# Prologue of a two-block transformer kernel: the first conditioning tiles in buffers of their own, their sums shared between TensorE and VectorE

## The reference, cut to what matters

```
c_act = jax.nn.silu(c)                          # (1, 1024)
mod = c_act @ w_ada[l] + b_ada[l]               # 6 x 1024 columns
sh1, sc1, gt1, sh2, sc2, gt2 = split(mod, 6)
h = rms_norm(x, norm1[l]) * (1.0 + sc1) + sh1
proj = h @ w_in[l]                              # the first large matmul
```

## Time and profile before

| | |
|---|---|
| median of 3 runs | 3449.75 us (3446.74 to 3453.58) |
| the profiled execution | 3449.55 us, of which the span in the trace is 3448.0 us |
| PE busy | 3332.4 us (97%), PEld 2752.0 us (80%) |
| DVE, ACT, POOL busy | 1887.3, 1107.1, 109.6 us |
| first dense matmul (L455) starts | 48.12 us into the span |
| mean granted clock of PE | 0.981 of full |

### The profile page before, as it was taken

How to read it: one execution, slowest core, us unless ns; L and a number is a source line. 1 busy time by engine, 2 the same in 40 slices (tenths; PEclk the granted TensorE clock), 3 DMA queues, 4 the chain that set the end, 5 groups by cost and what they waited for, 6 DMA issues and landing times.

```text
span 3448.0 us, 45974 instructions
## 1 busy us (share of the span) xinstructions
PE 3332.4 (97%) x15492; PEld 2752.0 (80%) x15492; DVE 1887.3 (55%) x2746; ACT 1107.1 (32%) x1465; POOL 109.6 (3%) x151
## 2 busy tenths in 40 slices
PE   5999999999999999999999999989999999999998
PEld 4788887888887788887888888668788878877887
DVE  7354557554446355577544443556575633566655
ACT  3233333322222333343322233253232323432322
POOL 1000000000000000000000000020000001000000
PEclk7999999999999999999999999999999999999999
DMA  6236424422222155325232222102222222012222
GB/s 224 68 122 207 140 91 148 145 92 97 97 97 87 48 172 183 123 92 195 92 103 94 96 77 84 63 25 75 97 91 98 92 94 89 32 62 97 92 92 79
DMA packets 98237, 357.84 MB, mean 104 GB/s; under 512 B 11104, under 2 KB 11120, under 8 KB 97856
## 3 DMA queue, kind: packets, MB, share of 16 engines
q1 hardware_dynamic: 97344, 353.73, 30.7%
q0 software_dynamic: 768, 2.47, 0.2%
HBM read 354.06 MB, written 2.10 MB: 103 GB/s over the span
## 4 chain that ended last, share of the span: by engine, by line
PE 84%; DVE 8%; DVEq 3%; issue 2%; ACT 2%; DMA 1%; ACTq 0%; SPq 0%; POOLq 0%
PE pb L428 22%; PE pb L429 21%; PE pb L430 21%; PE pb L491 2%; PE pb L492 2%; PE pb L493 2%; PE pb L455 2%; PE pb L456 1%; PE pb L459 1%; DVEq L1730 1%; PE pb L573 1%; DMA raw<-stream 1%; PE pb L506 1%; PE pb L873 1%; DVE act L1731 1%
## 5 line engine op out<-in xcount | busy, mean ns | idle before, releaser
L1331 DVE TENSOR_TENSOR lo<-raw,hi 128x1024 fp32r<-128x1024 f32 x549 | 681.6, 1246 | 449.9 <-ACT hi L938 386.6
L428 PE MATMUL pb<-hH,hi 128*128 128x512 f32 x2208 | 865.7, 392 | 13.9 <-DVE lo L1331 10.7
L429 PE MATMUL pb<-hL,hi 128*128 128x512 f32 x2208 | 862.7, 391 | 0.0
L430 PE MATMUL pb<-hH,lo 128*128 128x512 f32 x2208 | 862.1, 390 | 0.0
L938 ACT ACTIVATE hi<-raw 128x1024 fp32r<-128x1024 f32 x549 | 577.6, 1055 | 698.9 <-PE pb L430 417.3
L428 PE MATMUL pb<-yH,hi 128*128 128x512 f32 x1344 | 526.7, 392 | 23.8 <-DVEq L1385 21.1
L429 PE MATMUL pb<-yL,hi 128*128 128x512 f32 x1344 | 525.4, 391 | 0.0
L430 PE MATMUL pb<-yH,lo 128*128 128x512 f32 x1344 | 525.2, 391 | 0.0
L428 PEld LDWEIGHTS pb<-hH,hi 128*128 128x128 f32 x2208 | 416.3, 189 | 102.1 <-issue 6.8
L430 PEld LDWEIGHTS pb<-hH,lo 128*128 128x128 f32 x2208 | 416.3, 189 | 86.5
L429 PEld LDWEIGHTS pb<-hL,hi 128*128 128x128 f32 x2208 | 416.4, 189 | 85.1
(11 more groups left out here) (284 smaller groups left out, 3415.2 us busy)
## 6 DMA issues: line engine op xcount, KB each, us to landing
raw<-stream SPq DMA_DIRECT2D x664, 512.0 KB, 3.3
x<-xT SPq DMA_DIRECT2D x1, 2048.0 KB, 9.3
outT<-act SPq DMA_DIRECT2D x8, 256.0 KB, 2.2
tab<-decay SPq DMA_DIRECT2D x1, 1024.0 KB, 5.5
scr<-ws POOLq DMA_DIRECT2D x2, 256.0 KB, 4.3
scr<-bs POOLq DMA_DIRECT2D x2, 256.0 KB, 4.8
tab<-tables POOLq DMA_DIRECT2D x1, 512.0 KB, 4.0
cst<-consts SPq DMA_DIRECT2D x1, 302.0 KB, 3.3
```

Of the source, the lines that this page charges most:

```text
L428: pe.matmul(out, whi, ahi, start=first, stop=False)
L429: pe.matmul(out, whi, alo, start=False, stop=False)
L430: return pe.matmul(out, wlo, ahi, start=False, stop=last)
L1331: dve.tensor_tensor(lo[:, s], raw[:, s], hi[:, s].bitcast(F32), ALU.subtract).then_inc(lo_ready, 1)
```

## The change

- The 16 first tiles leave the stream and become an array `first` of their own. Each lands in memory that is unused so early: tiles 0 to 7 in `yF`, 8 to 15 in `act3` behind the squares. None waits for a slot. Each has its own semaphore. SP issues tiles 0 to 7, then 3 dense tiles, then tiles 8 to 15, then the rest of the stream.
- Even tiles of `first` are the transposed scale tiles, summed by DVE as before. Odd tiles are the shift weights in their plain layout, and PE makes a shift column from 8 matmuls, with 128 x 128 of the tile as weights and one column of c_act as moving operand, into PSUM bank 3; DVE copies the 8 columns to `mod`.
- The first norm is summed by PE alone (32 matmuls in place of 12); POOL's part is left out at this place.
- ACT makes the root and the sines before the three `hi`; `round_h` at the head of a layer (both layers) makes hH 0 and 1 before `tick(0)`.

```diff
-TILES = N_FIRST + LAYERS * LAYER_TILES + ...
+TILES = LAYERS * LAYER_TILES + ...
+        def first_at(n):
+            if n < 8:
+                return yF[:, n * TILE:(n + 1) * TILE]
+            return act3[:, KT + 2 * (n - 8):KT + 2 * (n - 8) + 2].rearrange("p a s -> p (a s)")
 ...
             sp.dma_start(x[:], xT).then_inc(x_in, 16)
             freed = Count()
-            early = N_FIRST + 3 * RING
+            for n in range(DENSE_AT):
+                sp.dma_start(first_at(n), first[n]).then_inc(first_in[n], 16)
+            early = 3 * RING
             for n in range(early):
+                if n == AHEAD:
+                    for m in range(DENSE_AT, N_FIRST):
+                        sp.dma_start(first_at(m), first[m]).then_inc(first_in[m], 16)
                 sp.wait_ge(lo_ready, freed.next())
                 sp.dma_start(raw[:, n % RING], stream[n]).then_inc(landed[n % RING], 16)
 ...
-            sum_squares()
+            sq.next(KT)
 ...
             spread_c()
-            norm_sum(start=True)
+            def shift_column(k):
+                pe.wait_ge(first_in[2 * k + 1], 16)
+                for j in range(KT):
+                    ins = pe.matmul(pb[:, 3, k:k + 1], first_at(2 * k + 1)[:, j * P:(j + 1) * P], cs[:, 1, j:j + 1],
+                                    start=j == 0, stop=j == KT - 1)
+                return ins
+            norm_sum(start=True, pooled=False)
+            for k in range(KT):
+                ins = shift_column(k)
+            ins.then_inc(shift_full, 1)
 ...
-            def round_h(shift=None):
+            def round_h(shift=None, tick_at=None):
                 for k in range(KT):
+                    if k == tick_at:
+                        tick(0)
                     act.wait_ge(h_scaled, hs.next())
 ...
-            for s in range(AHEAD):
-                split.next()
-                act.wait_ge(landed[(DENSE_AT + s) % RING], 16 * ((DENSE_AT + s) // RING + 1))
-                act.activation(hi[:, s], raw[:, (DENSE_AT + s) % RING], ACT.Copy).then_inc(hi_ready, 1)
             act.wait_ge(setup_in, 16)
             root(then_tick=False)
 ...
+            for s in range(AHEAD):
+                split.next()
+                act.wait_ge(landed[s], 16)
+                act.activation(hi[:, s], raw[:, s], ACT.Copy).then_inc(hi_ready, 1)
 ...
-                tick(0)
-                round_h(mod[:, 0:8])
+                round_h(mod[:, 0:8], tick_at=2)
 ...
-            for n in range(N_FIRST + AHEAD):
-                d = n - DENSE_AT
-                if 0 <= d < AHEAD:
-                    dve.wait_ge(hi_ready, split.next())
-                    dve.tensor_tensor(lo[:, d], raw[:, n % RING], hi[:, d].bitcast(F32), ALU.subtract).then_inc(lo_ready, 1)
-                else:
-                    m = n if d < 0 else n - AHEAD
-                    dve.wait_ge(landed[n % RING], 16 * (n // RING + 1))
-                    ada_sum(n % RING, mod[:, m:m + 1])
-                if n == 14:
-                    rstd()
+            def scale_column(k):
+                w = first_at(2 * k).rearrange("p (a e) -> p a e", a=2)
+                dve.wait_ge(first_in[2 * k], 16)
+                dve.tensor_tensor_reduce(w, w, c_all, 1.0, 0.0, ALU.mult, ALU.add, mod[:, 8 + k:9 + k])
+            for k in range(4):
+                scale_column(k)
+            rstd()
             for s in range(AHEAD):
+                dve.wait_ge(hi_ready, split.next())
+                dve.tensor_tensor(lo[:, s], raw[:, s], hi[:, s].bitcast(F32), ALU.subtract).then_inc(lo_ready, 1)
                 land[s].next(16)
+            for k in range(4, KT):
+                scale_column(k)
+            dve.wait_ge(shift_full, 1)
+            dve.tensor_copy(mod[:, 0:8], pb[:, 3, 0:8])
+            dve.drain()
             dve.wait_ge(trig, 2)
```

More of the change, by code:

```diff
@@ L33 @@
 N_FIRST = 16
-DENSE_AT = 9
+DENSE_AT = 8
 LAYER_TILES = N_ADA + 8 * 8 + 3 * 16 + 4 + 8 * 7
@@ L37 @@
 FFN2_TILES = 2 * sum(SLABS) + 8 * len(SLABS)
-TILES = N_FIRST + LAYERS * LAYER_TILES + (16 + 8 + 8 + FFN2_TILES) + (12 + 12 + 12 + 4 + FFN2_TILES)
+TILES = LAYERS * LAYER_TILES + (16 + 8 + 8 + FFN2_TILES) + (12 + 12 + 12 + 4 + FFN2_TILES)
 C_ID, C_PERM, C_ONES, C_CAUSAL, C_EDGE = 0, P, 2 * P, 3 * P, 4 * P
@@ L83, in repeat, with build @@
         c.n, c.off = n + k * trips, off
-def build(nc, stream, xT, cvec, pos, consts, decay, tables, vec1, ws, bs, vec2, wf, outT):
+def build(nc, stream, first, xT, cvec, pos, consts, decay, tables, vec1, ws, bs, vec2, wf, outT):
     with ExitStack() as ctx:
@@ L230, in build @@
         landed = [sem(f"landed{s}") for s in range(RING)]
+        first_in = [sem(f"first_in{n}") for n in range(N_FIRST)]
+        shift_full = sem("shift_full")
         hi_ready = sem("hi_ready")
@@ L418, in _ @@
         def _(pe):
-            tiles, banks = Count(4 + N_FIRST), Count()
+            tiles, banks = Count(4), Count()
             h_k, y_k, half_k = Count(), Count(), Count()
@@ L922, in _ @@
             split, done, stf = Count(), Count(4), Count()
-            land = [Count(N_FIRST // RING * 16) for _ in range(RING)]
+            land = [Count() for _ in range(RING)]
             ring = {split: RING, done: RING, **{c: 16 for c in land}}
@@ L2027 @@
     stream = np.concatenate(parts)
-    stream = np.concatenate([ada[0][0:DENSE_AT], stream[0:AHEAD], ada[0][DENSE_AT:N_FIRST], stream[AHEAD:]])
+    first = pairs_of(ada[0][8:16], tiles_t(a["w_ada"][0][:, 0:D]))
     assert stream.shape == (TILES, P, TILE), stream.shape
@@ L2038 @@
     data = {
-        "stream": stream,
+        "stream": stream, "first": first,
         "xT": np.ascontiguousarray(a["x"][0].T.reshape(KT, P, S).transpose(1, 0, 2)),
```

## The result

The changed kernel takes 3465.95 us in the median of six runs (3461.90 to 3467.99), the kernel before 3448.22 in six of the same series; the ratio is 1.0047, 95% interval 1.0036 to 1.0058. It is slower, by 12 to 20 us.

A forecast was written before the change was run, and what follows sets the result against it. PE's dense work was taken to bound the kernel, so the first dense matmul's shift from 48.12 to 61.2 us, mainly PE's 192 half-clock passes, gave +13.1 us: about 3463, range 3457 to 3468.

The forecast's parts named there:

- First tiles without slots: Start: first tiles come at the DMA rate, last landing at 38.1 or 44.0; old bound 44.16 falls by up to 6 us.
- The norm: First norm on PE alone: 64 passes at 0.214 us, done at 25.65, root 27.25, refined 28.3, spread done 30.0.
- Shift columns: PE behind the spread: 128 passes at 0.214 us, 27.4 us, from 30.0 to 57.6, hiding the stream's gain.
- The two readings that decided for 0.214 us a pass: One-column passes: clock stays 0.50 through 5.28 us at 19.73, and falls to 0.50 inside 64 passes from 2050.90.
- Copy and DVE's list: After the columns: copy to 57.85, 1.82 us to first scaled x, 1.56 to the first dense matmul at 61.2.
- Edits at nothing: DVE's other scale columns and lo, the tick behind hH 1, and early ws and bs loads: all costed at 0.
- The rival that the clock comes up: PE's one-column sums reach full clock after 3.6 us: first dense matmul 43.5, time 3443 to 3445; chance 0.09.
- the same dense tiles run in the same order, so I take a shift of that moment as the shift of the end: Whole kernel behind the start: the first dense matmul's shift, +13.1 us, was taken as the end's shift.
- in layer 1 hH already waits for DVE, not for the tick, so nothing changes there: Head of layer 1: moving the tick behind hH 1 was claimed to change nothing.

The follow-up runs named there:

- the run with landing alone: The change with all 16 sums on DVE, ACT's three hi and DVE's three lo ahead of the root: 3445.64 us against 3449.22 before, ratio 0.9991.
- the four traces with wide passes: Shift columns moving 128 copies (3454.78 us), these plus 16 matmuls (3453.01), and all sums on DVE, lists reordered, plus 24 (3442.87) or 34 (3442.55) unused 128-column matmuls.
- its second run: The changed kernel itself, unaltered, run once more: 3465.11 us against 3447.25 for the kernel before, ratio 1.0048.
- the one with POOL's norm: The change with POOL again adding squares 0 to 5 and PE making 12 norm matmuls, not 32: 3464.03 us against 3448.16 before, ratio 1.0042.
- the two with wide columns: The change with each shift-column pass moving 128 copies: 3454.78 us, ratio 1.0015 to before; the same plus 16 matmuls of 128 columns: 3453.01, ratio 1.0008.
- the run with four columns on PE: The change with shift columns 4 to 7 on DVE and 0 to 3 on PE: 3447.95 us against 3448.16 before, ratio 1.0000.
- with PE kept busy: The change with 128-copy shift columns and 16 more 128-column matmuls behind them: 3453.01 us against 3449.22 before, ratio 1.0008.
- the runs with 24 and 34 extra matmuls: All sums on DVE, lists reordered, plus unused 128-column PE matmuls from first tile 12's landing: 24, 3442.87 us, ratio 0.9980; 34, 3442.55, 0.9983 (to before).

## Why the prediction was right

The forecast was slower, 3463 us, with 3457 to 3468; it came out at 3465.95. The mechanism is the one forecast. The loss is 17.7 us where the sum had 13.1: the start came out to 0.3 us, and what is missing lies behind it. Step by step:

- **First tiles without slots.** The last first tile was to land at 38.1, at the latest 44.0. The DMA engines ran at 408 GB/s from 30 to 40 us and had nothing left by 42; in the run with landing alone DVE began the last sum at 39.06 without waiting. Hidden behind PE, as said; and worth 4.5 us, with the two lists put in order, where PE is not in the way.
- **The norm.** Sums from 11.73 to 25.54 (forecast 11.8 to 25.65), spread at 28.26 (28.3).
- **Shift columns.** The term on which all hung: 27.3 us from 30.13 to 57.43, forecast 27.4 from 30.0 to 57.6. The two readings that decided for 0.214 us a pass were right. By the Trainium skill's rule that activity releases the throttle (TensorE: Matmul & The Clock Gate, Part 1) the clock should have come up: PE was busy without a break for 13.8 and for 29.2 us and stayed at 0.50. In the four traces with wide passes the clock did come up, 2.8 to 5.9 us after their start.
- **Copy and DVE's list.** The copy took 0.17 and L1528 began 0.25 behind it, as forecast. From L1528 to the first scaled x it took 2.26 us, not 1.82: 0.66 us idle in front of L1567 where the trace of before had 0.22 at that step. (The same step comes back, larger, below.) DVE was done by 39.5, not 42, which changes nothing. From there to the matmul 1.55 (1.56). First dense matmul 61.53, forecast 61.2.
- **Edits at nothing.** The tick behind hH 1 cost nothing to be seen, ws and bs at 3.2 us did not delay x (it had landed at 11.0, before at 11.1). So the interleaving of loads that the Trainium skill describes (DMA: Bandwidth & Descriptors, Issuing engines are not separate DMA queues) cost x nothing here.
- **The rival that the clock comes up.** It did not, and no run brings it up in one-column passes. Its prices were near what the wide passes took: 0.112 us a pass for its 0.11, and 2.8 to 3.3 us of half speed first (5.9 in one trace) for its 3.6. With the shift columns alone wide the first dense matmul came to 50.21; the rival's 43.5 took both groups of sums at the full clock. One of its sums is off: at 0.14 us a pass the gain is not nil. By its own sum PE makes 200 passes up to the dense work (64, 8 and 128) and the rest of the path is 18.35 us, so the first dense matmul would be at 46.4, and the gain is nil at 0.149.

**What was mis-sized.** The medians differ by 17.7 and 17.9 us, the first dense matmuls by 13.4. So some 3 to 4 us of the loss are not in the chain that was summed: the step "the same dense tiles run in the same order, so I take a shift of that moment as the shift of the end". So is "in layer 1 hH already waits for DVE, not for the tick, so nothing changes there". At the head of layer 1 DVE stands in the chain, and it pauses there longer than before. Before, where the earlier trace rows has the instructions around it:

```profile
1047.66 0.17 DVE L1535 TENSOR_TENSOR bpps<-v 128x8 f32 x1 [0.20 <-issue]
```

in the change,

```profile
1061.40 0.18 DVE L1561 TENSOR_TENSOR mod<-mod,v 128x16 f32<-128x16 f32 x1 [3.30 <-issue]
1063.58 0.17 DVE L1567 TENSOR_TENSOR bpps<-v 128x8 f32 x1 [2.01 <-issue]
1065.90 0.60 PE L469 MATMUL pb<-hH,hi 128*128 128x512 f32 x1 [2.54 <-ACT hH L1044]
```

and in its second run

```profile
1063.58 0.17 DVE L1567 TENSOR_TENSOR bpps<-v 128x8 f32 x1 [1.98 <-issue]
1065.90 0.80 PE L469 MATMUL pb<-hH,hi 128*128 128x512 f32 x1 [5.23 <-ACT hH L1044]
```

The pause of 0.20 us has become 2.0, and from this instruction to the first hH and PE's matmul the steps take the same time in all three traces: 1.8 us of loss. (PE's own wait, 2.5 or 5.2 us, tells nothing of it: where PE makes the sums before it at half speed, it comes later and waits less.) The five traces with all eight shift columns on PE, the two of the change, the one with POOL's norm and the two with wide columns, have 1.88 to 2.02 us here; the other six have 0.20. At the same instruction in layer 0 it is 0.66 against 0.22, the 0.44 us of above. Counted from the first dense matmul, PE runs the same 15444 passes in all these kernels; from pass 4400 to 4500, which holds this place, the five take 22.7 to 23.8 us and the six 19.3 to 21.8, and no stretch of 100 passes elsewhere parts the two groups by over 0.1 us.

Neither the clock nor PE's work in the columns makes the pause: wide and narrow columns have it alike, and the run with four columns on PE has not. What the five share is DVE's program, 2731 instructions in the profile against 2739 and 2746. That the pause hangs on where this instruction stands in that program is argued, not shown; no run moves it by itself.

**What stays open.** First dense matmul and pause together are 15.2 us for the change, where the medians have 17.7 and 17.9 and the pooled means 16.8; 14.9 for the run with POOL's norm, which measured 15.9; 3.9 for the wide columns (6.6), and with PE kept busy 3.5 less the 1.8 of the half-speed stretch, so 1.7 (3.8). What is left, 1 to 3 us each, is inside every one of these intervals. It is all on one side, which may be chance: the clock differs from execution to execution at other places by as much. Between 2055 and 2257 us of the kernel before, the same 1000 passes take 199.3 us in one trace of the change and 201.4 in the other; most of that are 40 passes near 2127 us, 4.6 us at a PEclk of 0.91 in the first and 6.7 at 0.68 in the second. The kernel before took 6.5 us for the same 40. This also is why the pair of profiled executions shows none of the 3 to 4 us (from the first dense matmul to the end of the span 3399.9 us before, 3399.0 after): the pause is in it, and this stretch at a higher clock hides it.

## What to carry to other kernels

Before moving small sums from a vector engine to an idle matmul engine, price them at the clock that this engine has at that place, from a row where it does the same thing; PE, idle for most of this prologue, was at half speed there and stayed so. Count passes: a product of 128 x 128 in float32 with one column was two passes and 0.43 us, so a column of 8 such products took 3.4 us on PE where DVE took 1.14, and the 8 columns that DVE could have taken in 9 us took 27. Split a change that frees one resource (here the slots) and loads another into its two halves and measure each: the first half with ACT's and DVE's lists put in order, and PE warmed by matmuls that nobody reads, gives 3442.55 us, 4.7 us below the kernel before, where the whole gave 18 above. And compare the rest of the kernel too, instruction by instruction: an edit of the start brought a pause of 1.8 us a millisecond later, at an instruction that it had not touched.

## What the runs showed of the hardware

- **The clock beside one-column and wide passes.** PE made one-column passes for 27 us without a gap and stayed at 0.50, and in the earlier trace rows the clock fell from 1.00 to 0.50 inside such passes. In four of the eleven traces the first 3 to 6 passes of the norm's sums, near 12 us, stood 0.11 us apart, and all behind them 0.213; in no trace did the spacing shorten inside one-column passes before the dense work. With 128 columns in each pass, at the same number of passes, it rose 2.8 and 3.0 us after the first of them, and in the runs with 24 and 34 extra matmuls 3.3 and 5.9. A pass took 0.213 us at the half clock with one column or with 128, and 0.11 at the full clock: the width was free.
- **The recorded clock can be wrong at the start of a trace.** In the second run of the change PEclk reads 1.00 where the first reads 0.50, with as many passes in the same time:

```profile
30.00:40.00 10.00, 10.00 (x49) 10.00 (x49) 8.06 (x11) 4.59 (x5) 0.00 (x0) 1.00 1.03 409
40.00:50.00 10.00, 10.00 (x48) 10.00 (x48) 0.00 (x0) 0.00 (x0) 0.00 (x0) 1.00 0.19 75
```

  So near the start the count of passes in a stretch is the witness, and a mean clock of 0.988 beside 0.980 of the same kernel says nothing about its speed.
- **SP took longer for an issue when many loads were under way.** It gave out the first 8 tiles at 0.5 us each, the 3 dense tiles at 1.85, the next 8 at 1.4 (0.524 MB each, so 380 GB/s, about the pace of landing). In the change it is not in the chain behind 12 us:

```profile
2.32 4.06 SPq L335 DMA_DIRECT2D yF<-first  x8
6.42 5.55 SPq L342 DMA_DIRECT2D raw<-stream  x3
12.02 11.05 SPq L340 DMA_DIRECT2D act<-first  x8
```
- **A pause of DVE of 1.8 us at one instruction, the same in five traces.** 0.20 us in six traces, 1.88 to 2.02 in five, at the head of the second pass of the layer loop; at the head of the first 0.22 and 0.66. Just before it, every trace has one of 3.3 to 3.5 us in the second pass and of 0.19 in the first. The profile names no releaser for any of them.
